# A long fused kernel on one core: two more gate tiles ahead of an attention's head loop, and a recurrence's factors made in the phase before it

## The reference, cut to what matters

```python
def dsa_mixer(x, ...):             # 16 heads of 128, one key and one value for all
    h = x @ w_in                   # q, k, v, gate z, indexer
    ...
    _, idx = lax.top_k(score, topk)
    logits = einsum('bthd,btjd->bthj', q_b, k_sel) * ATTN_SCALE
    probs = softmax(where(valid, logits, -inf))
    o = einsum('bthj,btjd->bthd', probs, v_sel)
    return (o * jax.nn.silu(z)) @ w_out

def rwkv7_time_mix(r, w_lo, k, v, a_lo, ...):   # 4 heads of 64
    decay = exp(-exp(w_log))
    a = sigmoid(a0 + a_lo @ a2)
    kk = k * k_k;  kk = kk / max(norm(kk), 1e-12)
    k = k * (1 + (a - 1) * k_a)
    def step(state, inp):
        sa = state @ -kk_t
        state = state * w_t + sa * (kk_t * a_t) + v_t * k_t
        return state, state @ r_t
    ...
    y = rms_norm(y) * ln_g + sum(r * k * r_k) * v
```

## Time and profile before

| what | value |
|---|---|
| median of 3 runs | 1563.53 us (1562.69 to 1565.89) |
| the profiled execution | 1566.23 us, span 1564.5 us |
| busy, share of the span | PE 94%, ACT 33%, DVE 42%, POOL 35% |
| mean granted clock of TensorE | 0.973 of full speed |
| DSA head loop | 735.61 to 902.4 us |
| branches | 1348 to 1410.4 us |
| rwkv_prep | 1410.8 to 1421.4 us |
| pair stage | 1421.8 to 1437.5 us |
| busy in the branches (62.5 us from 1348) | DVE 39.55, ACT 26.18, POOL 23.82 us |
| busy in the pair stage (16 us from 1421.5) | DVE 14.86, ACT 5.61, PE 7.66 us |

### The profile page before, as it was taken

One profiled execution on the slowest core, in us unless ns is written; L12 is line 12 of the kernel. 1 busy time (PEld: TensorE's weight loads), 2 busy tenths in 40 slices (PEclk: granted clock), 3 DMA queues, 4 the chain that ended last, 5 costly groups with the idle time before them and its releaser, 6 DMA issues. The chain is left out here.

```text
span 1564.5 us, 24852 instructions
## 1 busy us (share of the span) xinstructions
PE 1472.7 (94%) x10701; PEld 1276.3 (82%) x10701; DVE 652.6 (42%) x1308; ACT 523.5 (33%) x862; POOL 551.9 (35%) x231
## 2 busy tenths in 40 slices
PE   7999999999998999997999899998999999787997
PEld 7898885999997987785888799788978887566887
DVE  6032440142216454497554501725117114567525
ACT  3345124333213323423434412234334324443210
POOL 6424421233332327852463224232333331231312
PEclk9999999999999999998999999999999999886999
DMA  5222320122521322222010142234332220002211
GB/s 167 81 81 81 98 64 27 40 96 81 202 81 55 109 88 81 81 84 79 28 54 29 54 176 81 82 95 132 90 103 86 81 81 0 1 0 82 75 37 54
DMA packets 113755, 121.29 MB, mean 78 GB/s; under 512 B 12529, under 2 KB 107613, under 8 KB 113390
## 3 DMA queue, kind: packets, MB, share of 16 engines
q1 hardware_dynamic: 110096, 113.77, 22.9%
q10 hardware_dynamic: 3550, 5.94, 1.0%
HBM read 113.41 MB, written 6.29 MB: 77 GB/s over the span
## 5 line engine op out<-in xcount | busy, mean ns | idle before, releaser
L193 POOL TENSOR_TENSOR w_low<-w_ring,w_high 128x2048 fp32r<-128x2048 f32 (+1 forms) x91 | 413.4, 4543 | 753.0 <-ACT w_high L184 752.8
L209 PE MATMUL ps<-w_high,xT_high 128*128 128x256 f32 (+1 forms) x1056 | 304.4, 288 | 9.2 <-POOL w_low L451 4.2
L209 PE MATMUL ps<-w_high,xT_low 128*128 128x256 f32 (+1 forms) x1056 | 298.7, 283 | 0.0
L209 PE MATMUL ps<-w_low,xT_high 128*128 128x256 f32 (+1 forms) x1056 | 298.5, 283 | 0.0
L184 ACT ACTIVATE w_high<-w_ring 128x2048 fp32r<-128x2048 f32 (+1 forms) x91 | 171.5, 1885 | 289.5 <-PE ps L209 285.1
L209 PE MATMUL ps<-xT_high,w_high 128*128 128x512 f32 (+1 forms) x600 | 241.0, 402 | 4.0 <-POOL w_low L193 3.0
L209 PE MATMUL ps<-xT_low,w_high 128*128 128x512 f32 (+1 forms) x600 | 238.1, 397 | 0.0
L209 PE MATMUL ps<-xT_high,w_low 128*128 128x512 f32 (+1 forms) x600 | 238.0, 397 | 0.0
L209 PEld LDWEIGHTS ps<-w_high,xT_high 128*128 128x128 f32 x1056 | 202.1, 191 | 17.3 <-issue 7.0
L209 PEld LDWEIGHTS ps<-w_low,xT_high 128*128 128x128 f32 x1056 | 202.3, 192 | 1.7 <-issue 1.7
L209 PEld LDWEIGHTS ps<-w_high,xT_low 128*128 128x128 f32 x1056 | 201.9, 191 | 0.0
(11 more groups left out here) (503 smaller groups left out, 2195.8 us busy)
## 6 DMA issues: line engine op xcount, KB each, us to landing
w_ring<-in_gla_w_in_dram SPq DMA_DIRECT2D x24, 1024.0 KB, 5.3
w_ring<-in_dsa_w_in_dram SPq DMA_DIRECT2D x19, 1024.0 KB, 5.2
w_ring<-in_w_in_dram SPq DMA_DIRECT2D x18, 1024.0 KB, 5.2
w_ring<-in_gla_w_out_dram SPq DMA_DIRECT2D x8, 1024.0 KB, 5.0
w_ring<-in_ple_gate_w_dram SPq DMA_DIRECT2D x8, 1024.0 KB, 4.9
w_ring<-in_dsa_w_out_dram SPq DMA_DIRECT2D x8, 1024.0 KB, 4.9
x_scratch<-x SPq DMA_DIRECT2D x4, 1024.0 KB, 6.8
w_ring<-in_w_out_dram SPq DMA_DIRECT2D x4, 768.0 KB, 4.8
```

Of the source, the lines that this page charges most:

```text
L193: self.nc.gpsimd.tensor_tensor(self.slot(self.w_low, i % RING, k, cols), self.slot(self.w_ring, n % RING, k, cols), self.slot(self.w_high, ...
L209: return self.nc.tensor.matmul(out, lhs, rhs, start=first, stop=last, skip_group_check=not check)
```

## The change

It has three parts.

1. **DSA.** n_early is 22. The two added tiles are projected before the head loop on PE and ACT; DVE takes its step for the first between mask(0) and mask(1), for the second behind mask(1). The other 10 tiles go by halves: heads 0 to 3 take two halves (a whole tile), heads 4 to 15 one half each. On PE all halves but a head's last stand behind turn_prob(h, 1), the last one behind turn_prob(h, 3), and turn_out(h-1) stands behind that. On DVE gate_out(h-1) stands behind copy_turned(h, 3).
2. **The factors.** at, rt, bt, kt and hats are written by DVE in the branches phase, over decay, decay_at, kk, log_decay, a_gate and grow. running_decay, decay_before and decays move earlier to make that possible. The block rwkv_prep is gone.
3. **The rwkv block.** at and rt no longer lie side by side, so the pairs are 16 products of 64x64 in place of 8 of 64x128. The pairs of at with bt use one pair of banks and wait for T_step. Bonus and token transposes follow each tile's pairs on PE, and ACT's copies of them stand ahead of mix_high. POOL's first split waits for all four T_init and goes in 4 instructions of 128x512.

```diff
-    def split_low(self, pool, upto=None):
+    def split_low(self, pool, upto=None, parts=1):
...
+            for a in range(parts):
+                part = slice(a * k // parts, (a + 1) * k // parts)
+                ins = self.nc.gpsimd.tensor_tensor(low[:, part], whole[:, part], high[:, part].bitcast(F32), ALU.subtract)
+            ins.then_inc(self.w_low_made, 1)
...
-        n_early = DSA_HEADS + n_silu
+        n_early = DSA_HEADS + n_silu + 2
+        late_halves = [(n_early + i // 2, i % 2) for i in range(2 * (n_tiles - n_early))]
+        two_each = len(late_halves) - DSA_HEADS
+        first_half = lambda h: 2 * min(h, two_each) + max(h - two_each, 0)
+        halves_of = lambda h: late_halves[first_half(h):first_half(h + 1)]
...
                     turn_prob(h, 0)
                     turn_prob(h, 1)
-                    if n_early + h < n_tiles:
-                        project(n_early + h, range(0, KD // 2))
+                    for n, half in halves_of(h)[:-1]:
+                        project(n, half_tiles[half])
+                    turn_prob(h, 2)
+                    turn_prob(h, 3)
+                    for n, half in halves_of(h)[-1:]:
+                        project(n, half_tiles[half])
                     if h:
                         turn_out(h - 1)
-                    turn_prob(h, 2)
-                    turn_prob(h, 3)
-                    if n_early + h < n_tiles:
-                        project(n_early + h, range(KD // 2, KD))
...
                     copy_turned(h, 1)
+                    copy_turned(h, 3)
                     if h:
                         gate_out(h - 1)
-                    copy_turned(h, 3)
...
                 mem_exps(1)
+                decays()
...
                 squares(1)
-                decays()
...
+                def inverse_factors():
+                    dve.wait_ge(sem["decays"], past["decays"] + 4)
+                    nc.vector.tensor_tensor(s.decay[:], s.kk[:], s.decay[:], ALU.mult).then_inc(sem["at"], add("at", 1))
+                    nc.vector.tensor_tensor(s.decay_at[:], s.shifted[:, 0:PAIRS, :], s.decay_at[:], ALU.mult).then_inc(sem["rt"], add("rt", 1))
...
                 copy_inputs(1)
+                running_decay()
                 peaks(0)
                 logs(1)
                 weighted(0, (0,))
+                decay_before()
...
                 logs(2)
-                running_decay()
+                inverse_factors()
                 peaks(2)
+                b_factor()
                 divided(0)
...
                 divided(1)
-                decay_before()
+                b_grown()
...
                 square_sums(1)
+                k_grown()
+                to_ends(0)
                 divided(2)
                 mem_out(3)
+                to_ends(1)
                 divided(3)
...
+                    for w, y_side in enumerate((at, rt)):
                         for i in range(PAIRS):
...
+                                    ins = g.product(ps[out, 2 * (n % 2) + b, (2 * i + w) * C:(2 * i + w + 1) * C], x[rows, i, toks], y_side[rows, i, toks])
...
+                for j in range(NT):
+                    pair(2 * j)
+                    pair(2 * j + 1)
+                    transposed_pair(j)
+                    if j == 0:
+                        bonuses()
+                    turn_tokens(2 * j)
+                    turn_tokens(2 * j + 1)
...
             def _(act):
-                g.split_high(act, w_out + 1)
+                for n, (which, j2) in enumerate(turns):
+                    act.wait_ge(sem["tok_turned"], past["tok_turned"] + n + 1)
...
+                    if n == 3:
+                        g.split_high(act, w_out + 1)
                 for tiles in early:
...
             def _(pool):
-                g.split_low(pool, w_out + 1)
+                pool.wait_ge(sem["T_init"], past["T_init"] + NT)
+                g.split_low(pool, w_out + 1, 4)
```

More of the change, by code:

```diff
@@ L1325, in phase_dsa @@
         n_silu = 4
-        n_early = DSA_HEADS + n_silu
+        n_early = DSA_HEADS + n_silu + 2
[3 more added lines that the diff above has]
+        halves_of = lambda h: late_halves[first_half(h):first_half(h + 1)]
+        half_tiles = (range(0, KD // 2), range(KD // 2, KD))
+        late_done = lambda h: [n for n, half in halves_of(h) if half == 1]
         score_tiles = range(1, NT)
@@ L1658, in _ @@
                 mask(0)
+                project(DSA_HEADS + n_silu)
                 mask(1)
+                for n in range(DSA_HEADS + n_silu + 1, n_early):
+                    project(n)
                 for h in range(DSA_HEADS):
@@ L2958, in phase_rwkv @@
-        g.sem.end_phase()
+        v_ = shifted[:, 2 * PAIRS:3 * PAIRS, :]
+        turns = [(which, j2) for which in (2, 3, 0, 1) for j2 in range(NT // 2)]
         y_in = lambda j: ps[:, 4:6, j * P:(j + 1) * P]
@@ L2967, in _, with pair @@
             def _(pe):
-                for j in range(NT):
-                    for a, x in enumerate((bt, kt)):
-                        n = 2 * j + a
-                        if n >= 2:
-                            pe.wait_ge(sem["pair_masked"], past["pair_masked"] + n - 1)
+                def pair(n):
+                    j, x = n // 2, (bt, kt)[n % 2]
+                    if n >= 2:
+                        pe.wait_ge(sem["pair_masked"], past["pair_masked"] + n - 1)
+                    for w, y_side in enumerate((at, rt)):
                         for i in range(PAIRS):
@@ L2985, in _, with bonuses, turn_tokens @@
                             for b, rows in enumerate(block_rows):
-                                ins = g.product(ps[out, 4 + 2 * (j % 2) + b, i * C:(i + 1) * C], ar[rows, i, j, 0, out], bt[rows, i, toks])
+                                ins = g.product(ps[out, 4 + b, i * C:(i + 1) * C], at[rows, i, toks], bt[rows, i, toks])
                     ins.then_inc(sem["L_ready"], add("L_ready", 1))
+                def bonuses():
+                    for j in range(NT):
+                        for i in range(PAIRS):
+                            ins = g.product(ps[:, 7, j * GH + 2 * i:j * GH + 2 * i + 2], s.rk[:, i, j * P:(j + 1) * P], g.same64[:, 0:P:HD])
+                    ins.then_inc(sem["bonus_ready"], add("bonus_ready", 1))
+                def turn_tokens(n):
+                    which, j2 = turns[n]
+                    if n == 1:
+                        pe.wait_ge(sem["bonus_copied"], past["bonus_copied"] + 1)
+                    elif n >= 2:
+                        pe.wait_ge(sem["tok_copied"], past["tok_copied"] + n - 1)
+                    for j in (2 * j2, 2 * j2 + 1):
+                        for i in range(PAIRS):
+                            at_col = (j - 2 * j2) * GW + i * P
+                            ins = nc.tensor.transpose(ps[:, 6 + n % 2, at_col:at_col + P], (hats[0], hats[1], v_, at)[which][:, i, j * P:(j + 1) * P], g.ident[:])
+                    ins.then_inc(sem["tok_turned"], add("tok_turned", 1))
+                for j in range(NT):
+                    pair(2 * j)
[5 more added lines that the diff above has]
+                    turn_tokens(2 * j + 1)
                 units = [(m, j) for m in range(1, LEVELS) for j in range(NT)]
@@ L3063, in across @@
                     for half, out in enumerate(block_rows):
-                        ins = g.product(ps[out, bank, at], ar[rows, h // 2, j, 1, out], state[rows, 2 * j + half, h // 2, :], False, half == 1, check=False)
+                        ins = g.product(ps[out, bank, at], rt[rows, h // 2, (2 * j + half) * C:(2 * j + half + 1) * C], state[rows, 2 * j + half, h // 2, :], False, half == 1, check=False)
                     ins.then_inc(sem["y_ready"], add("y_ready", 1))
```

116 lines of the change are left out of this document (42 added, 74 removed).

## The result

The changed kernel takes 1553.63 us, median of 4 runs (1551.94 to 1555.25), beside 1564.71 of the kernel before in its 4 (1562.69 to 1566.13): ratio 0.9923, 95% interval 0.9907 to 0.994, so 9 to 15 us less. The profiled execution has a span of 1553.3 against 1564.5, 11.2 less. 1555 was forecast.

A forecast was written before the change was run, and what follows sets the result against it. PE was taken as the bound nearly everywhere, so gains come from filled waits or shorter half-clock stretches. DSA -4.1 and branches with pair stage -4.6 make -8.7, from a median of 1563.5 to 1555 us; range 1549.0 to 1560.8.

The forecast's parts named there:

- The sum: Whole kernel: -4.1 us from the DSA part and -4.6 from branches and pair stage, -8.7 in all, median 1555.
- The start of the loop: Ahead of the head loop: two added tiles fill PE's 11.07 us wait and keep full clock; loop starts 1.06 earlier.
- Heads 1 to 3: Head loop, heads with a whole tile: later gate_out delays the mask, 0.39 us more each, 12.15 per head.
- Heads 4 to 13: Head loop, heads with one half tile and logits: 10.06 us each, the fourth turn waiting for DVE's second copy.
- Heads 14 and 15: End of the head loop, heads with a half tile and no logits: 7.3 us each.
- The third rival: Head loop: bound by its uncovered chain; waits double to 2.4 us, a head takes 11.3, total +3.4, 1567; chance 0.09.
- Branches: Branches phase: decays leave ACT's path, 0.8 to 1.0 us less on PE; added DVE products cost 0.
- The pair stage: Factor stage up to the first doubling copy: -4.6 us, branches' 0.9 included; half clock to about 1421, mix_high then exposed.
- The first rival: Pair stage: clock stays at half, total -4.4, 1559, chance 0.22; or rises early, gain 8, 1551, chance 0.08.
- The fourth rival: Doubling behind the pair stage: starts at full clock instead of half, up to 2 us more gained, 1553; chance 0.06.
- L3203: Pair stage: DVE instruction taking 4.57 us beside POOL's weight split is freed by the later split; contained in the sum.
- the second rival: Branches: a new DVE product waits for POOL; price up to 2.4 us, 1557.4; chance 0.10.

The follow-up runs named there:

- e7: Changed kernel with its half tiles, but the output's turn and gate_out back in the order of the kernel before; 0.9877 of the kernel before (one run), loop 158.15 us.
- e3: Changed kernel with the ten late tiles whole on heads 0 to 9 and the old order within a head; 0.9877 of the kernel before, loop 157.79 us.
- e1: Kernel before with the DSA part of the change alone; 0.998 of the kernel before.
- e12: Kernel before with each factor pair as 16 products of 64x64 instead of 8 of 64x128, nothing else; 0.9987 of the kernel before (one run).
- e8: Changed kernel with whole tiles on heads 0 to 9, keeping its new order within a head; 0.9913 of the kernel before (one run), loop 161.81 us.
- e10: Changed kernel with halves in the old order, mix_high between token copies and POOL's first split behind DVE's third mask; 0.9847 of the kernel before.
- e4: Changed kernel with ACT's three mix_high copies and the weight's split set between the token copies; 0.9907 of the kernel before, block 18.42 us.
- e6: Changed kernel with POOL's first split whole and without its wait, as before the change; 0.995 of the kernel before (one run), block 23.28 us.
- e5: Changed kernel with mix_high and the split between token copies, and POOL's first split waiting for DVE's third mask; 0.9884 of the kernel before.

## Why the prediction was right, and where its sizes were off

**The sum.** -8.7 was forecast (the loop's own sum is 165.9 - 163.0 = 2.9, put down as 3.0). The traces show -11.2, the medians -11.1 and the interval of the ratio -9 to -15: the forecast's side, and 1553.63 lies inside its range. That 1555 came so near is partly luck: the DSA part gave 1.0 less than forecast (-3.1 for -4.1), branches and factor stage 3.8 more (-8.4 for -4.6), and the median of the kernel before rose by 1.2 with its fourth run.

**The start of the loop** was right in size (-1.0 for -1.06) and in cause: no 11 us wait, full clock, but the chain of logits and masks, with DVE's step for the added tile between the two heads' masks, kept the rest, as the prediction had it. ACT's first exponential comes 3.0 us later behind the choice of keys than before (3.6 against 0.6); that was not foreseen, and it held nothing up here.

**Heads 1 to 3** were right: 12.15 forecast, 12.13 to 12.15 measured, with the mask's wait as the cause. **Heads 4 to 13** were right: 10.06 forecast, 10.13 measured, 0.7 over ten heads. Heads 14 and 15 take 7.37 for 7.3 (5.50 before), though the prediction's reason for that figure does not add up from rows 4. The loop took 164.71 where 166.82 less 3.0 was forecast, so the -3.0 became -2.1: 0.7 by the ten heads, the rest at the end. Where its mechanism was wrong is the sentence on the 8.2 us that "come back as waits that whole tiles hid". 9.1 came back (11.2 of work less the 2.1), and by e7, which keeps the halves, 6.6 of them are the new order's; the halves by themselves cost 0.4 (e7 against e3). Most of it, 0.39 for the mask in 13 heads or 5.1, stood in the prediction's own sum, but it was not called a price of the order or weighed against leaving the order alone. The third rival, the chain without cover, exists at the size of the forecast and not doubled: 10.13 less 8.88 of work is 1.25 per head, of which 0.51 goes with the order (e7's 9.62).

**Branches.** PE's wait for the turned memory probabilities is gone (it has no row among PE's waits there any more), and the new DVE products of 128x1024 took what they should: 1.21 to 1.22 each, one of them 1.48 beside POOL. Where the 0.6 by which the phase is shorter comes from can't be said. With the old branches it took 62.2 (before), 62.3 (e1) and 61.3 (e12), with the new ones 61.2 to 63.5 in eleven kernels. The mean granted clock of the phase differs too: 0.79 before, 0.86 in the changed kernel, 0.76 in the two longest (e8 and e10). The -0.9 is therefore neither shown nor refuted. The pair of block ends that goes was put at about 0.4; the trace before has a wait of PE of 1.13 there, ahead of the first pair (1421.78), which is gone.

**The pair stage** is where the largest term was mis-sized: "The price of a tile at half clock: two pairs of 16 products, each twice the 0.65". 0.65 is the busy time of a group, in which the tails of its last matmuls are contained; the step from one group to the next is 0.43 at half clock and 0.235 at full. A tile had cost 5.15 or 3.46 by the forecast and takes 4.2 at half (the first, without the bonus) and 2.35 at full clock (the third) in the trace, so the turns ended 15.7 us after the stage's first product and not 19.7: that is the 4 us. The section on time and profile before had the warning in it (busy is longer than the step), and the forecast used it for the tiles of DSA and not here. The half clock lasted about 10 us, near the 11 that were assumed, but not for the reason given: the 12 us read from rows 9 are the width of that row's window. In that trace the granted clock is 0.50 from 1418 to 1419 and 0.99 from 1419 to 1420, so it rose 8 us behind prep's first product (1410.82). mix_high then stood on the path with its 3.8, as forecast, but only 1.9 of it held the first copy back, and e4, which moves it away, shortens the block by 2.0: DVE's masks, which the prediction had keeping up, stand right behind it. The first rival fell with its slow side, half clock throughout; its fast side has the size that came out (8 for 8.4) but another cause, since the clock did not rise early. The fourth rival held for the doubling's first two groups and then fell: the clock was 0.52 from 1428 to 1430, and the doubling is 0.4 shorter, which is within its scatter.

**L3203** was right in kind, but had no price: the prediction has it "contained in the sum". By e6 the hold and the four parts are worth 2.9 together.

**POOL and DVE in the branches** (the second rival). inverse_factors' second product took 1.48 in place of 1.22 beside POOL's masks, which took 3.69. That is hardly more than before: there the same masks took 3.56 beside running_decay, where other such groups take 1.7. The kernel before, then the changed one:

```profile
1374.94 3.56 POOL L2711 TENSOR_TENSOR branch_room<-branch_room,not_before 128x128 f32<-128x128 f32 x4 [6.88 <-ACT branch_room L2643]
```

```profile
1374.47 1.48 DVE L2814 TENSOR_TENSOR decay_at<-raw,decay_at 128x1024 f32<-128x1024 f32 x1
```

```profile
1372.99 3.69 POOL L2723 TENSOR_TENSOR branch_room<-branch_room,not_before 128x128 f32<-128x128 f32 x4 [6.72 <-ACT branch_room L2655]
```

```profile
1387.18 1.22 DVE L2822 TENSOR_TENSOR late<-late,grow 128x1024 f32<-128x1024 f32 x1
```

```profile
1386.09 3.75 POOL L2740 TENSOR_SCALAR rk<-raw,cols 128x512 f32<-128x512 f32 x2
```

So the rival's price was 0.3 on DVE, not 2.4; whether PE felt it is not shown. By the Trainium skill, "SBUF — State Buffer", section "Who interferes with whom", a DVE instruction with two SBUF inputs contends with a GpSimd instruction that reads SBUF. The trace agrees where POOL's instruction has two inputs (3.69, and 4.97 in e6), and it does not where POOL's has one: b_grown ran its normal 1.22 inside POOL's two TENSOR_SCALARs of 3.75 in sum. The measurement decides.

## What to carry to other kernels

Price a group of matmuls by the distance between the starts of neighbouring groups at the clock in question, never by its busy time. Where a PE order has a necessary wait, put it where it lets other engines' copies finish (here the output's turn between the two pairs of turns, after a wait of 0.46). With the turn and DVE's gate_out moved behind the work, that wait came back as 0.24, 0.18 and 0.33 elsewhere, and the head took 0.51 longer. Look at the whole stage after moving work into a gap of ACT or POOL: e4 took 2.0 off the block and lost 1.7 of it in the doubling, where the clock fell to 0.50; e5, with one wait of PE fewer, had 1.00 there and kept 2.8.

## What the runs showed of the hardware that was not expected

- A single DVE instruction was stretched from 0.69 to 4.97 us by one POOL instruction of 4.54 (e6), and POOL's four parts took 5.42 in sum beside DVE's three masks, which took 3.23 in place of 1.2 (e4): in four parts the loss is shared instead of lying on one engine.
- 32 products of 64x64 take as long as 16 of 64x128: 0.91 at half clock, and 0.60 at full in the one group that can be compared (e12).
- The same code takes different times in different executions: the new branches 61.2 to 63.5, the stretch from the head loop to the branches 444.9 to 448.0, the time ahead of DSA 1.4 apart in the first two traces. The head loop, at full clock throughout, repeats within 0.1, so only comparisons within a stage could resolve the small terms.
